# Two transformer blocks on one core: the order of transposes and value products in the first block's attention

## The reference, cut to what matters

```python
p = jnp.exp(scores - m)
p = p / (jnp.sum(p, axis=-1, keepdims=True) + jnp.exp(sink - m))
o = jnp.einsum('bngrqk,bnkgd->bnqgrd', p.astype(v.dtype), vc)
...
p_s = masked_softmax(s_s.reshape(b, g, r, BLOCK, n_sel * SLC_LEN), mask_s)
o_s = jnp.einsum('bgrqn,bgqnd->bqgrd', p_s.astype(v_slc.dtype), ...)
...
p_w = masked_softmax(s_w, mask_w)
o_w = jnp.einsum('bgrqk,bkgd->bqgrd', p_w.astype(vwin.dtype), vwin)
return gt[..., 0:1] * o_c + gt[..., 1:2] * o_s + gt[..., 2:3] * o_w
```

## Time and profile before

| | |
|---|---|
| time, median of 3 runs | 1697.22 us (1696.67 to 1697.7) |
| the profiled execution: its own time | 1696.4 us |
| its span, first to last instruction | 1694.6 us |
| TensorE busy | 1678.5 us, 99% |
| VectorE, ScalarE, GpSimd busy | 72%, 61%, 41% |
| TensorE clock granted | 1.00 in all slices |
| attention of the first block, layer 1 and 2 | about 88 to 131 us and 459 to 502 us |
| share of the chain that ended last | PE 96%, DVE 3%, ACT 1% |

### The profile page before, as it was taken

One profiled execution on the slowest core, in us unless ns is written; L12 is line 12 of the kernel. 1 busy time (PEld: TensorE's weight loads), 2 busy tenths in 40 slices (PEclk: granted clock), 3 DMA queues, 4 the chain that ended last, 5 costly groups with the idle time before them and its releaser, 6 DMA issues.

```text
span 1694.6 us, 25929 instructions
## 1 busy us (share of the span) xinstructions
PE 1678.5 (99%) x9650; PEld 1437.0 (85%) x9650; DVE 1221.3 (72%) x1840; ACT 1026.9 (61%) x1901; POOL 694.9 (41%) x672
## 2 busy tenths in 40 slices
PE   8999999999999999999999999999999999999998
PEld 7868888889868988889888979888898889788887
DVE  8877799958868899957664757665576647576663
ACT  5687766645786766655553657554565536575543
POOL 4154167602046166507660052673066600517640
PEclk9999999999999999999999999999999999999999
DMA  8925486576807576649756625866496575358662
GB/s 243 246 67 169 132 235 186 174 223 177 210 16 214 160 204 180 220 141 249 191 182 223 203 96 155 230 175 219 141 246 181 188 231 195 104 145 216 186 212 75
DMA packets 416353, 306.70 MB, mean 181 GB/s; under 512 B 10180, under 2 KB 369014, under 8 KB 416227
## 3 DMA queue, kind: packets, MB, share of 16 engines
q1 hardware_dynamic: 415536, 304.51, 61.6%
q0 software_dynamic: 688, 0.53, 0.1%
q10 hardware_dynamic: 2, 0.00, 0.0%
HBM read 303.95 MB, written 1.05 MB: 180 GB/s over the span
## 4 chain that ended last, share of the span: by engine, by line
PE 96%; DVE 3%; ACT 1%; issue 0%; DMA 0%; SPq 0%; DVEq 0%; ACTq 0%
PE bank L1550 34%; PE bank L1553 17%; PE bank L1664 9%; PE bank L1665 9%; PE bank L1666 9%; PE bank L1627 3%; PE bank L1624 3%; PE bank L1616 3%; PE bank L1597 1%; PE bank L1875 1%; PE bank L1845 1%; PE bank L1586 1%; PE bank L1588 1%; PE bank L1587 1%; DVE PB L1226 1%; PE bank L1768 1%
## 5 line engine op out<-in xcount | busy, mean ns | idle before, releaser
L970 DVE TENSOR_TENSOR whl<-raw,whl 128x1024 fp32r<-128x1024 f32 (+2 forms) x572 | 738.8, 1315 | 169.6 <-ACT whl L601 165.3
L1550 PE MATMUL bank<-hsA,whl 128*128 128x512 f32 x2384 | 762.7, 397 | 0.0
L601 ACT ACTIVATE whl<-raw 128x1024 fp32r<-128x1024 f32 (+2 forms) x572 | 575.4, 1029 | 159.7 <-PE bank L1666 102.1
L1553 PEld LDWEIGHTS bank<-hsA,whl 128*128 128x128 f32 x2384 | 448.0, 188 | 101.3
L1553 PE MATMUL bank<-hsA,whl 128*128 128x256 f32 x2384 | 472.9, 278 | 0.0
L1550 PEld LDWEIGHTS bank<-hsA,whl 128*128 128x128 f32 x2384 | 369.3, 189 | 4.8 <-issue 2.9
L601 ACT ACTIVATE low<-bank 128x256 f32<-128x256 f32 x390 | 144.6, 376 | 276.4 <-PE bank L1550 256.8
L1415 POOL TENSOR_TENSOR HB<-CB,UB 128x256 f32<-128x256 f32 x88 | 123.6, 1405 | 338.0 <-ACT CB L604 337.3
L1664 PE MATMUL bank<-whl,hid 128*128 128x512 f32 x528 | 205.9, 390 | 0.0
L1666 PE MATMUL bank<-whl,hid 128*128 128x512 f32 x528 | 205.5, 389 | 0.0
L1665 PE MATMUL bank<-whl,hid 128*128 128x512 f32 x528 | 205.4, 389 | 0.0
(11 more groups left out here) (228 smaller groups left out, 2014.6 us busy)
## 6 DMA issues: line engine op xcount, KB each, us to landing
raw<-in_ffn_w_up SPq DMA_DIRECT2D x176, 512.0 KB, 5.2
raw<-in_ffn_w_down SPq DMA_DIRECT2D x120, 512.0 KB, 4.6
raw<-in_w_in SPq DMA_DIRECT2D x96, 512.0 KB, 6.1
raw<-in_ffn_w_gate SPq DMA_DIRECT2D x88, 512.0 KB, 4.0
raw<-in_w_out SPq DMA_DIRECT2D x32, 512.0 KB, 4.6
raw<-in_ffn_w_down SPq DMA_DIRECT2D x24, 256.0 KB, 3.0
G<-in_norm_g SPq DMA_DIRECT2D x12, 512.0 KB, 6.8
raw<-in_cmp_w SPq DMA_DIRECT2D x8, 512.0 KB, 5.8
```

Source lines behind the costliest of these rows:

```text
L601: return nc.scalar.activation(out_, in_, func, **kw)
L970: v.tensor_tensor(wlo[c_ % RING][:, x:y], raw[:, c_ % RAW, x:y], whi[c_ % RING][:, x:y].bitcast(F32), ALU.subtract)\
L1550: return mm(out_[:, 0:2 * n], whi[slot][:, at:at + P], rhs[:, 0:2 * n], start=x == 0, stop=False, **g32)
L1553: return mm(out_[:, n:2 * n], wlo[slot][:, at:at + P], rhs[:, 0:n], start=False, stop=False, **g32)
```

## The change

On TensorE alone, and from step 10 of the loop on, the order of T and V is another. Until step 9 all is as before. At step 10 both T(6) and T(7) stand after S(10), then V(5). From step 12 on an even step i holds S(i), T(i-4), T(i-3), V(i-6), V(i-5), and an odd step holds nothing of them. The waits are the same, each still in front of its own T or V. The other engines' instructions and their order are the same.

```diff
--- before.py
+++ after.py
@@ -187,6 +187,18 @@
 
 MAPS = [(u, 0) for u in range(6)] + [(u, b) for u in range(6) for b in (1, 2)]
 LAST_MAP = list(range(6)) + [7 + 2 * u for u in range(6)]
+
+
+def turned_at(i):
+    if i < 6 + SKEW:
+        return [i - SKEW] if i >= SKEW else []
+    return [m for m in (i - SKEW, i - SKEW + 1) if i % 2 == 0 and m < len(MAPS)]
+
+
+def valued_at(i):
+    if i < 7 + SKEW:
+        return [i - SKEW - 1] if i > SKEW else []
+    return [m for m in (i - SKEW - 2, i - SKEW - 1) if i % 2 == 0 and m < len(MAPS)]
 
 
 def build(nc, a, out):
@@ -1829,8 +1841,7 @@
                     early_tile(3, i // 2)
                 if i == 2:
                     cmp_scores()
-                m = i - SKEW
-                if 0 <= m < len(MAPS):
+                for m in turned_at(i):
                     nh = len(UNITS[MAPS[m][0]][2])
                     nk = 4 // nh
                     pe.wait_ge(probs_ready, done + m + 1)
@@ -1845,13 +1856,12 @@
                             ins = nc.tensor.transpose(bank[6 + m % 2][:, (kb * nh + x) * P:(kb * nh + x + 1) * P],
                                                       PB[:, m % RINGP, (x * nk + kb) * P:(x * nk + kb + 1) * P], ident)
                     ins.then_inc(pt_ready, 1)
-                if m == 0:
+                if i == SKEW:
                     pe.wait_ge(cmp_p, L + 1)
                     for qb in range(2):
                         ins = nc.tensor.transpose(bank[7][:, qb * P:qb * P + P], PC[:, qb, :, :].rearrange("p h c -> p (h c)"), ident)
                     ins.then_inc(cmp_t, 1)
-                m = i - SKEW - 1
-                if 0 <= m < len(MAPS):
+                for m in valued_at(i):
                     u, br = MAPS[m]
                     g, qb, hs = UNITS[u]
                     nh = len(hs)
```

## The result

The changed kernel takes 1701.77 us (median of 9 runs, 1701.25 to 1702.78), against 1696.96 us for the kernel before in the same comparison (9 runs): ratio 1.0027, 95% interval 1.0019 to 1.0036. It is 4.8 us slower. The prediction was 1701.1 us.

The account below looks back on a forecast made before the run. TensorE was taken to bound the attention stretch. Per layer, waits of 3.89 us less 1.92 us of changeovers gave +1.97, +3.9 in all, so 1697.2 would go to 1701.1 us; 8-in-10 range 1698.2 to 1702.8.

Parts of the forecast that it names:

- TensorE bounds the stretch: Attention steps at 109 to 133 us and in the second layer: TensorE has no idle time, so its time reaches the total.
- A change of kind: TensorE switching between full-array transposes and half-array value products: 0.16 us each, 12 fewer per layer, 1.92 us less.
- the sum: Per layer, S(10) to M1: waits 3.89 us, changeovers -1.92, giving +1.97 us; +3.9 us in both layers.
- The copies wait for the postponed V: On ScalarE, C(m) needs V(m-2), now later; C(8) starts over 1 us later in relation to TensorE.
- The six waits: TensorE ahead of T(11) 0.76, T(13) 0.93, T(14) 0.33, T(15) 1.21, T(16) 0.33, T(17) 0.33 us; 3.89 per layer.
- the walk: First layer's new order stepped through from T(6) to M1 with the earlier trace's durations, to find TensorE's waits.
- The hops: Signal delays between engines: 0.06 us to TensorE, 0.03 to ScalarE; 0.14 to TensorE would add 1.0 us in all.
- the walk's own last line: M1 in the first layer at 133.27 where it was 131.20: +2.07 us, the difference put down to rounding of changeovers.
- Rival 1: ScalarE has room enough in the stretch, so only the changeovers count: faster, 1693.4 us; chance 0.08.
- Rival 2: Only part of TensorE's waits appear, T(13) waiting only for C(11): 1700.2, or 1698.2 without the 0.33 waits; chance 0.20.
- Rival 3: On TensorE the wait costs the changeover, not the kind, so pairs save nothing: 1702.7 us; chance 0.09.
- rival 4: Nothing changes because TensorE's order does not matter: 1697.2 us; chance 0.03.

Follow-up runs that it names:

- e7: Kernel before with 24 changeovers added, V's compressed products placed between transposes of T(m+1); 1700.84 us, ratio 1.0022 against before.
- e8: Changed kernel with four places for copies and another order: T(12), T(13), T(17) regrouped, T(15) with T(16); 1693.50 us, ratio 0.9979 against before.
- e1: Changed kernel with four places for the copies in PT instead of two, so C(m) waits for V(m-4); 1697.20 us, ratio 1.0001 against before.
- e5: Kernel before, its order kept, with four places for the copies instead of two; 1697.19 us, ratio 1.0000 against before.
- e4: Changed kernel with the wait for the copies written ahead of the wait for the probabilities before each T; 1702.19 us, ratio 1.0028 against before.
- e2: Kernel before with only T in pairs, V one by one where it was; 1695.15 us, ratio 0.9987 against before.
- e3: Kernel before with only V in pairs one step later, T one by one where it was; 1695.94 us, ratio 0.9992 against before.

## Why the prediction was right, and what was mis-sized

- **TensorE bounds the stretch, and all of it reaches the end.** Right: the excess of T(6) to M1, twice, is the measured difference within 0.3 us in every kernel, and both layers agree within 0.02 us.
- **A change of kind costs 0.16 us, 12 fewer per layer.** Right: 0.15 by e7 and by e8, so 1.85 us per layer where the sum had 1.92. A pair costs nothing at its boundary: T(8) and T(9) take 115.39 - 114.37 = 1.02 us for 2 x 0.43 + 0.16.
- **The copies wait for the postponed V.** Shown by e1 with its control e5, and by ScalarE: ahead of C(8) its row has 1.00 us of idle time that TensorE's line 1885 ended, where it was 0.65 by line 1845.
- **The six waits.** All where they were put, 4.30 us by starts for the 3.89 of the sum. By distances between starts, the walk against the trace: T(10) to T(11) 1.19 and 1.34 us; T(12) to T(13) 1.36 and 1.34; V(10) to T(14) 1.57 and 1.72; T(14) to T(15) 1.64 and 1.63; V(12) to T(16) 1.78 and 1.94; T(16) to V(14) 1.35 and 1.33.
- **The hops were mis-sized.** The forecast had +1.97 us per layer, the trace +2.40. The 0.43 us are the three chains V, C, T that are 0.15 or 0.16 us longer than walked: T(11), T(14), T(16). They make 0.46, the other three distances are 0.05 shorter, and the rest is rounding. (Against the walk's own last line, +2.07, the miss is 0.33, since the walk's pieces make a changeover 0.15 us.) Of each, 0.08 is the hop from the copy to T, 0.14 in place of 0.06 (the prediction named 0.14 as an upper bound, for all six waits; e4 shows what it hangs on). The rest is the hop from V's result to the copy: V(6) to C(8) took 116.59 - 115.39 = 1.20 us, walked as 1.12, and V(10) to C(12) 0.98, walked as 0.91. V's semaphore is the second of the copy's two waits, which fits e4, but the swap was not tried on ScalarE. T(15) and T(17) follow a C that follows a C, so the error cancels.
- **The row ahead of T(16)** names GpSimd's PB as the releaser. P(16) was done at 127.08 + 1.09 = 128.17 (the row of GpSimd under e4); it was C(14), 129.13 + 0.60 = 129.73, 0.14 us ahead of T(16). With the waits swapped (e4), the same row names ACT PT. The prediction has T(16) wait for C(14), which holds; its size, 0.33 us, and that of T(14) were too small, 0.49 and 0.48 by starts, and T(17)'s was 0.31.
- **Rivals.** Rival 1, that ScalarE has room, fell on the distance it was said to hang on: from C(8)'s start to C(9)'s result ScalarE took 119.10 - 116.59 = 2.51 us, walked as 2.53, where TensorE would have been at T(11) after 1.8. Its share of busy time did not matter. Rival 2 had a point only in that P(13) is not a full wait of its own: with the copies free 0.67 us of the 0.91 by starts is left (e1). Rival 3 is out by e7, rival 4 by the measured difference.

## What to carry to other kernels

Grouping instructions of one kind on TensorE was worth 0.15 us here for each change between 128*128 and 128*64 saved, but only as long as nothing that frees a buffer moved behind what asks for it. Before moving a reader (V) later, follow its buffer: who refills it (C), what that engine has queued behind it (E), and when the refill's user (T) now comes; a shift by one map gave most of the saving (e2), an extra pair of places alone only took the loss away (e1), and the places with a matching order gave all of it (e8). An engine's busy share did not show this (ScalarE had 5 us of 24 free); the distance from release to need did.

## What the runs showed of the hardware that was not expected

- Of two waits in front of one TensorE instruction, the one written first releases it 0.04 to 0.06 us after its signal, the one written second 0.14 to 0.15 us after (changed kernel and e4, both ways round).
- T(17) and M0 stand side by side in e8: both use the full array, though one is a transpose and the other a matmul. M0 starts 0.42 us after T(17), the four transposes' own time; in e3 it is 0.41 us. So the changeover went with the array's shape and not with the kind of work. This is shown between 128*128 and 128*64; the price of a change to or from the scores' 64*128 was not measured by itself.
